# Side products woven into the quarters of each weight slab in a hybrid decoder layer

## Chip, cores and metric

One NeuronCore of a Trainium2 chip runs the whole layer in one launch. The metric is the device time of the launch in microseconds (us), as the median of several runs. The engines are called PE (TensorE), DVE (VectorE), ACT (ScalarE), POOL (GpSimd) and SP (SyncE, which issues most of the transfers).

## The reference

One decoder layer for 512 tokens of width 1024, all in float32. A normalised input `h` goes through one wide projection; its parts feed two token mixers, whose outputs are gated, summed and projected, and a squared-ReLU MLP follows:

```python
proj = h @ w_in[l]
(hq, hf, hi, hg, cq, ak, av, ik, iw, gate_a, gate_b) = jnp.split(proj, splits, axis=-1)
oa = hgrn2_mixer(hq, hf, hi, lbs[l])           # 4 heads of 128: S_t = diag(f_t) S_t-1 + (1 - f_t) i_t^T, o_t = S_t^T q_t
oa = rms_norm(oa, hgrn_norm_g) * jax.nn.silu(hg)
cq = rms_norm(cq, q_norm_g[l])
aq = cq @ w_uq[l]                              # 8 attention heads of 64
iq = cq @ w_iq[l]                              # 8 index heads of 64
ik = layer_norm(ik, ...)
ob = dsa_mixer(aq, iq, iw, ak, av, ik, rel_bias)   # score = sum_h w_h relu(iq_h . ik); top 128 keys; softmax(q.k + bias) v
mix = jax.nn.sigmoid(gate_a) * (oa @ w_up_hgrn[l]) + jax.nn.sigmoid(gate_b) * (ob @ w_up_attn[l])
x = x + mix @ w_o[l]
x = x + jnp.square(jax.nn.relu(hm @ w_mlp_in[l])) @ w_mlp_out[l]
```

## The kernel before

Each engine's instruction stream is written out by hand, and the engines meet at semaphores only: `full[b]` and `free[b]` count the uses of each of the eight PSUM banks, and named semaphores (`kk_done`, `iqh_done`, `e_done`) count steps. Float32 products are made of three fast matmuls (`three`, lines 1445 to 1447): each operand is split into a high part, rounded by a cast on ACT (`whi`, line 637), and a low part, the difference, made on DVE (`wlo`, line 956).

The weights come as slabs of 128 by 1024 numbers in the order of `PLAN`, 55 of them before the MLP. The text numbers them from 0: slabs 0 to 3 are hf, 4 to 7 hq, 8 to 11 c0, 12 c1, 13 to 16 hi, 17 iq (the index queries), 18 to 21 hg, 22 uq (the attention queries), 23 to 30 ga, 31 to 34 ua (the recurrence's up-projection), 35 to 42 gb, 43 to 46 ub and 47 to 54 wo. There are four slots for slabs. Each slab is 24 matmuls of 512 columns (of 384 in iq). The slabs write the PSUM banks 0 to 3 in rotation; everything else, the side products, writes banks 4 to 7.

The table `side[n]` names the side steps that belong to slab n; the same table drives every engine. Each engine's loop over the slabs is:

- PE: the 24 matmuls of the slab (`mms`), then the PE part of the slab's side steps.
- ACT: the high part of slab n + 3 (`hi`), then the ACT parts of the side steps, then what it does with the slab's own result (`evict`); for the slabs in `EARLY`, among them 17 (iq), 21 (hg 3) and 22 (uq), evict stands ahead of the side steps.
- DVE: the steps `diff`, `dput`, `put` of the slab, then the low part of slab n + 3 (`lo`), then side steps and evict in the same way.

The side steps that the text names:

- `mul` 0 to 6: products of the recurrence by levels; `xm` makes their operands on DVE (lines 1153 and 1154), `put` copies results into `hA`.
- `kdT`: transposes of the attention keys (`kdh`, `kdl`), and before the change also of the index keys (`ikd`, line 1088, then `ikh` on ACT and `ikl` on DVE).
- `decay_k`: DVE writes the exponents (line 1188), ACT takes the exp (line 770). `use_k` multiplies the keys `hK` by them on DVE (line 1195) and raises `kk_done`. `kT` 0 to 2 transposes `hK` on PE, the first waits for `kk_done`. `decay_q`, `use_q` and `turn` are the same for queries and `hA`. `state` and `out` are the recurrence by chunks.
- `index` 0 to 23: two matmuls, a relu on ACT and an accumulation on DVE (line 1100). `top`: one round of the top-k selection on DVE (lines 1110 and 1113), 16 rounds for each of the token tiles 1, 2 and 3.
- `on`: 16 multiplications on DVE (line 1224); `flip` and `oaT` are matmuls and transposes for what follows.
- `attn` 0 to 34, the attention of 32 (token tile, head) pairs as a pipeline: step u multiplies queries and keys of pair u on PE, adds the bias and takes the minimum on DVE (line 1241), takes the exp on ACT (line 826), transposes the pair u - 2 on PE, copies it on ACT, and multiplies the pair u - 3 by the values on PE (line 1668). Pair u - 3 lands in columns 0 to 63 of bank 7, and DVE scales it into `ob` (lines 1249 and 1252) before the next pair may be written.

Of the kernel before, what the change touches and what calls it, by code (L numbers as in the profile page):

```python
# [25 lines left out]
P = 128  # L26
# [26 lines left out]
        + [("hg", j) for j in range(4)] + [("uq", 0)] + [("ga", j) for j in range(8)] + [("ua", j) for j in range(4)]  # L53
# [21 lines left out]
def build(nc, x, slabs, vecs, consts, onehot, rel_bias, final_g, out):  # L75
    with ExitStack() as ctx:
# [6 lines left out]
        def sem(name):  # L83
# [37 lines left out]
        ikd = place("ikd", 165, T)  # L121
        ikh = place("ikh", 167, T, F32R)
# [77 lines left out]
                 "rsum_done obh_done mix_done mxh_done mxl_done hv_done hh_done hl_done fin_done rq_done "  # L200
# [89 lines left out]
        file(n_de - 1, ("decay_k",))  # L290
        file(n_de, ("put", LEVELS - 1), ("use_k",), ("decay_q",))
        file(n_de + 1, ("use_q",), ("turn",))
# [3 lines left out]
        file(n_hi + 3, ("kdT",))  # L296
        n_ch = n_de + 2
# [41 lines left out]
        N_TOP = n_top  # L339

# [289 lines left out]
        def _(act):  # L630
# [38 lines left out]
            def evict(n):  # L669
# [61 lines left out]
            def do_side(s):  # L731
# [79 lines left out]
                if k == "attn":  # L811
                    u = s[1]
                    bq, btp, bv = BK[s]
                    if btp is not None:
# [3 lines left out]
                        if v >= 2:  # L818
                            wait_full(BK["attn", v + 1][2])
# [1031 lines left out]
```

## Time and profile before

| | us |
|---|---|
| median of 3 runs (765.9 to 767.69) | 766.44 |
| the profiled execution, its own time | 767.56 |
| its span | 765.8 |
| PE busy in the span | 731.8 (96%) |
| DVE busy | 548.1 (72%) |
| ACT busy | 354.2 (46%) |

The span is the time from the first to the last instruction on the core; the profiled execution's own time is 1.8 us more. A busy PE is one that has a matmul in it; it says nothing of how fast the matmul ran.

### The profile page before, as it was taken

What the parts mean: (1) busy time and instruction counts of PE and PEld (TensorE: products, weight loads), DVE (VectorE), ACT (ScalarE), POOL (GpSimd) and SP (SyncE); (2) the same over time, 40 slices, a digit from 0 to 9 for tenths busy, and PEclk for the clock granted to TensorE, in tenths of its full rate; (3) what the DMA queues carried; (4) which work ended last, traced back from release to release, by engine and by line L of the source; (5) the groups of instructions that cost most, each with busy time, mean ns of one, the idle gap of its engine ahead of it and who ended that gap; (6) DMA issues with size and microseconds to landing.
All of it is one profiled execution on the core that took longest, in us unless ns stands there. A gap on an engine that the chain in (4) does not pass through costs nothing.

```text
span 765.8 us, 9945 instructions
## 1 busy us (share of the span) xinstructions
PE 731.8 (96%) x3498; PEld 609.8 (80%) x3498; DVE 548.1 (72%) x868; ACT 354.2 (46%) x572; POOL 84.0 (11%) x121
## 2 busy tenths in 40 slices
PE   5999999898898999999999999999999999999996
PEld 4788888687676778888888888888888888888885
DVE  4587997658999896433842677695959596868974
ACT  6463454555534334443322664535445454545442
POOL 5021330011001133420010100000000000000002
PEclk9999999899999999999999999999999999999998
DMA  7521221111222112111261515060413233241102
GB/s 286 160 89 56 69 96 56 56 55 56 84 82 83 56 56 83 56 56 56 89 244 52 195 60 185 1 194 25 164 55 129 90 101 118 82 138 55 56 1 110
DMA packets 20724, 71.51 MB, mean 93 GB/s; under 512 B 2344, under 2 KB 3536, under 8 KB 20688
## 3 DMA queue, kind: packets, MB, share of 16 engines
q1 hardware_dynamic: 19120, 67.88, 26.4%
q10 hardware_dynamic: 1568, 3.15, 1.2%
q8 instruction: 22, 0.36, 0.2%
q14 instruction: 14, 0.11, 0.0%
HBM read 68.91 MB, written 2.11 MB: 93 GB/s over the span
## 4 chain that ended last, share of the span: by engine, by line
PE 82%; DVE 13%; issue 2%; DMA 1%; ACT 1%; POOL 0%; SPq 0%; POOLq 0%; DVEq 0%
PE bank L1445 25%; PE bank L1446 24%; PE bank L1447 24%; DVE sc L1113 2%; PE bank L1668 2%; DVE small L1110 2%; DVE wlo L956 2%; PE bank L1453 1%; PE bank L1572 1%; DMA xs<-x 1%; DVE sc L1100 1%; DVE aqs L1006 1%; PE bank L1652 1%; PE bank L1653 1%; DVE hO L1224 1%
## 5 line engine op out<-in xcount | busy, mean ns | idle before, releaser
L1445 PE MATMUL bank<-hTh,whi 128*128 128x512 f32 (+1 forms) x456 | 181.1, 397 | 1.5 <-DVE hTl L976 1.5
L1447 PE MATMUL bank<-hTh,wlo 128*128 128x512 f32 (+1 forms) x456 | 178.8, 392 | 0.0
L1446 PE MATMUL bank<-hTl,whi 128*128 128x512 f32 (+1 forms) x456 | 178.6, 392 | 0.0
L1445 PEld LDWEIGHTS bank<-hTh,whi 128*128 128x128 f32 (+1 forms) x456 | 86.1, 189 | 21.3 <-issue 1.9
L956 DVE TENSOR_TENSOR wlo<-raw,whi 128x1024 fp32r<-128x1024 f32 x58 | 72.2, 1247 | 41.9 <-ACT whi L637 41.9
L1447 PEld LDWEIGHTS bank<-hTh,wlo 128*128 128x128 f32 (+1 forms) x456 | 85.8, 188 | 18.7
L1446 PEld LDWEIGHTS bank<-hTl,whi 128*128 128x128 f32 (+1 forms) x456 | 86.0, 189 | 18.2 <-issue 0.5
L637 ACT CAST whi<-raw 128x1024 fp32r<-128x1024 f32 x58 | 60.4, 1043 | 34.7 <-PE bank L1447 34.5
L1445 PE MATMUL bank<-whi,ah 128*128 128x512 f32 x196 | 76.2, 389 | 0.0
L1446 PE MATMUL bank<-wlo,ah 128*128 128x512 f32 x196 | 76.2, 389 | 0.0
L1447 PE MATMUL bank<-whi,al 128*128 128x512 f32 x196 | 76.2, 389 | 0.0
L871 ACT ACTIVATE rt<-bank 128x512 f32<-128x512 f32 x32 | 19.1, 598 | 85.9 <-PE bank L1447 85.9
L862 ACT CAST whi<-raw 128x1024 fp32r<-128x1024 f32 x29 | 29.8, 1052 | 50.3 <-PE bank L1447 50.3
L1292 DVE TENSOR_TENSOR wlo<-br,whi 128x1024 fp32r<-128x1024 f32 x32 | 39.0, 1220 | 18.8 <-ACT whi L867 18.6
L1325 DVE TENSOR_TENSOR acc<-bank,acc 128x512 f32<-128x512 f32 x70 | 44.9, 682 | 0.0
L1445 PE MATMUL bank<-whi,hTh 128*128 128x512 f32 x96 | 39.3, 410 | 3.8 <-DVE iqs L1006 3.8
L1447 PEld LDWEIGHTS bank<-whi,al 128*128 128x128 f32 x196 | 36.8, 188 | 7.7
L1445 PEld LDWEIGHTS bank<-whi,ah 128*128 128x128 f32 x196 | 36.8, 188 | 7.6
L1446 PEld LDWEIGHTS bank<-wlo,ah 128*128 128x128 f32 x196 | 36.8, 188 | 7.6
L1292 DVE TENSOR_TENSOR wlo<-raw,whi 128x1024 fp32r<-128x1024 f32 x29 | 34.8, 1219 | 10.4 <-ACT whi L862 10.4
L820 ACT ACTIVATE et<-bank 128x128 f32<-128x128 f32 (+3 forms) x32 | 14.0, 436 | 58.9 <-PE bank L1453 58.5
L1446 PE MATMUL bank<-wlo,hTh 128*128 128x512 f32 x96 | 38.5, 401 | 0.0
(231 smaller groups left out, 1360.6 us busy)
## 6 DMA issues: line engine op xcount, KB each, us to landing
raw<-slabs SPq DMA_DIRECT2D x87, 512.0 KB, 3.4
br<-slabs SPq DMA_DIRECT2D x32, 512.0 KB, 3.4
xs<-x SPq DMA_DIRECT2D x4, 512.0 KB, 5.4
y<-x ACTq DMA_DIRECT2D x1, 2048.0 KB, 8.9
out<-ys SPq DMA_DIRECT2D x3, 512.0 KB, 2.6
bt<-bias_rows ACTq DMA_DIRECT2D x1, 1024.0 KB, 5.3
cst<-consts SPq DMA_DIRECT2D x1, 608.0 KB, 9.7
fg<-final_g SPq DMA_DIRECT2D x1, 512.0 KB, 7.2
```

Source lines behind the costliest of these rows:

```text
L637: act.copy(whi[s][:, :], raw[s][:, :]).then_inc(hi_done, 1)
L862: act.copy(whi[s][:, :], raw[s][:, :]).then_inc(hi_done, 1)
L871: act.activation(rt[m % 2][:, :], bank[m][:, :], ACT.Relu).then_inc(free[m], 1)
L956: dve.tensor_tensor(wlo[s][:, :], raw[s][:, :], whi[s][:, :].bitcast(F32), ALU.subtract).then_inc(lo_done, 1)
L1110: dve.max(mx8[:, 8 * (i - 1):8 * i], sc_of(i)).then_inc(S["max_done"], 1)
L1113: dve.match_replace(sc_of(i), mx8[:, 8 * (i - 1):8 * i], sc_of(i), TAKEN).then_inc(S["rep_done"], 1)
L1292: dve.tensor_tensor(wlo[s][:, :], src[:, :], whi[s][:, :].bitcast(F32), ALU.subtract).then_inc(lo_done, 1)
L1325: dve.tensor_tensor(a_, bank[b][:, :], a_, ALU.add).then_inc(free[b], 1)
L1445: pe.matmul(dst, lh, rh, start=start, stop=False)
L1446: pe.matmul(dst, lh, rl, start=False, stop=False)
L1447: return pe.matmul(dst, ll, rh, start=False, stop=stop)
L1668: ins = pe.matmul(bank[7][:, 0:DH], et[v % 2][:, q * P:(q + 1) * P], c03[:, q, QL + GR * DH + g * DH:QL + GR * DH + (g + 1) * DH], start=q ...
```

## The change

- Every slab is cut into four parts of six matmuls each. After each part stands a share of the slab's side steps (`woven[n][p]`), on PE, ACT and DVE alike. Steps that need a bank are laid at even distances; the `top` rounds of a slab are spread over its parts. `evict` is cut in the same way, and `EARLY` is gone.
- The keys' decay moves: `decay_k` from the DVE work of slab 15 to that of slab 16, behind `kdT`; `use_k` and `decay_q` from slab 16 to the end of slab 17; `use_q` from 17 to 18. The index keys are a step of their own (`iknT`) in slab 17, with other places in memory, and no longer wait for `use_k`.
- `ga` 0 comes before `uq`: uq is now slab 23. The 24 index steps stand in slabs 18 to 21. The 35 attention steps begin at slab 31 (ua 0) and not at slab 28; they still end in slab 40. The rounds of `top` for tile 2 stand in slabs 25 to 31 (before: 23 to 29), those of tile 3 in 31 to 35 (before: 28 to 34).
- The eight heads of a token tile share bank 7: pair (i, h) is written to columns 64h to 64h + 63, and once per token tile one reciprocal of 8 columns and one multiplication of 512 columns move all of it to `ob`. PE waits for that (`ob_done`) only at the first head of the next token tile.

The diff, cut to its core (`evict`, `token_part` and `feature_part` are cut into four parts in the same way as the loops at its end):

```diff
-        + [("hg", j) for j in range(4)] + [("uq", 0)] + [("ga", j) for j in range(8)] + [("ua", j) for j in range(4)]
+        + [("hg", j) for j in range(4)] + [("ga", 0), ("uq", 0)] + [("ga", j) for j in range(1, 8)] + [("ua", j) for j in range(4)]
...
-        ikd = place("ikd", 165, T)
-        ikh = place("ikh", 167, T, F32R)
+        ikd = place("ikd", 197.5, T)
+        ikh = place("ikh", 195, T, F32R)
...
-        file(n_de - 1, ("decay_k",))
-        file(n_de, ("put", LEVELS - 1), ("use_k",), ("decay_q",))
-        file(n_de + 1, ("use_q",), ("turn",))
...
+        file(n_iq, ("iknT",))
+        file(n_de, ("put", LEVELS - 1), ("decay_k",))
+        file(n_de + 1, ("turn",), ("use_k",), ("decay_q",))
+        file(n_de + 2, ("use_q",))
...
-        spread([("index", u, i, h) for u, (i, h) in enumerate(idx_units)], n_hg, n_uq)
+        spread([("index", u, i, h) for u, (i, h) in enumerate(idx_units)], n_hg, n_hg + 3)
         file(max(n_hg + 3, n_ch + NT), ("bt", ))
-        file(n_ga, *[("on", c) for c in range(NT)])
-        spread([("flip", h) for h in range(AH // 2)], n_ga + 2, n_ga + 4)
-        file(n_ga + 4, ("oaT",))
-        spread([("attn", u) for u in range(NU + 3)], n_ga + 5, n_gb + 5)
-        spread([("top", (1,), r_) for r_ in range(rounds)], n_hg + 2, n_ga + 1)
-        spread([("top", (2,), r_) for r_ in range(rounds)], n_ga, n_ga + 6)
-        file(n_ga, ("mask", 0))
-        file(n_ga + 2, ("mask", 1))
-        file(n_ga + 7, ("mask", 2))
-        spread([("top", (3,), r_) for r_ in range(rounds)], n_ga + 5, n_gb - 1)
-        file(n_gb, ("mask", 3))
+        file(n_uq, *[("on", c) for c in range(NT)])
+        spread([("flip", h) for h in range(AH // 2)], n_ua - 6, n_ua - 4)
+        file(n_ua - 4, ("oaT",))
+        spread([("attn", u) for u in range(NU + 3)], n_ua, n_gb + 5)
+        spread([("top", (1,), r_) for r_ in range(rounds)], n_hg + 2, n_ua - 7)
+        spread([("top", (2,), r_) for r_ in range(rounds)], n_ua - 6, n_ua)
+        file(n_ua - 6, ("mask", 0), ("mask", 1))
+        file(n_ua + 1, ("mask", 2))
+        spread([("top", (3,), r_) for r_ in range(rounds)], n_ua, n_gb)
+        file(n_gb + 1, ("mask", 3))
         file(n_gb + 6, ("obT",))
 
-        EARLY = (n_hi + 3, n_iq, n_uq, n_hg + 3)
...
+                    if u == 3:
+                        pv_bank = take(7)
...
+        PARTS = 4
+        woven = {}
+        for n in range(NPLAN):
+            woven[n] = [[] for _ in range(PARTS)]
+            count = sum(s in BK for s in side[n])
+            tops = sum(s[0] == "top" for s in side[n])
+            seen, p, top = 0, 0, 0
+            for s in side[n]:
+                if s in BK:
+                    p = (2 * seen + 1) * PARTS // (2 * count)
+                    seen += 1
+                if s[0] == "top":
+                    woven[n][top * PARTS // tops].append(s)
+                    top += 1
+                else:
+                    woven[n][p].append(s)
...
             for n in range(NPLAN):
                 hi(n + AHEAD)
-                if n in EARLY:
-                    evict(n)
-                for s in side[n]:
-                    do_side(s)
-                if n not in EARLY:
-                    evict(n)
+                for p in range(PARTS):
+                    evict(n, p)
+                    for s in woven[n][p]:
+                        do_side(s)
                 for s in side[n]:
                     if s[0] == "out":
...
-                    if bv is not None:
-                        v = u - 3
-                        i, h = units[v]
-                        dve.wait_ge(S["e_done"], v + 1)
-                        if v >= 2:
-                            dve.wait_ge(free[7], BK["attn", v + 1][2][1] + 1)
-                        dve.reciprocal(resum[:, v % 2:v % 2 + 1], esum[:, v:v + 1]).then_inc(S["rsum_done"], 1)
-                        wait_full(bv)
-                        dve.wait_ge(S["rsum_done"], v + 1)
-                        dve.tensor_scalar(ob3[:, i, h * DH:(h + 1) * DH], bank[7][:, 0:DH], resum[:, v % 2:v % 2 + 1],
-                                          None, ALU.mult).then_inc(free[7], 1)
+                    if bv is not None and units[u - 3][1] == AH - 1:
+                        i = units[u - 3][0]
+                        e_ = esum[:, AH * i:AH * i + AH]
+                        dve.wait_ge(S["e_done"], AH * (i + 1))
+                        dve.reciprocal(e_, e_).then_inc(S["rsum_done"], 1)
+                        if i < NT - 1:
+                            dve.wait_ge(S["pv_done"], AH * (i + 1))
+                        else:
+                            wait_full(bv)
+                        dve.wait_ge(S["rsum_done"], i + 1)
+                        dve.tensor_tensor(ob3[:, i, :].rearrange("p (h d) -> p h d", h=AH),
+                                          bank[7][:, :].rearrange("p (h d) -> p h d", h=AH),
+                                          e_.unsqueeze(2).to_broadcast([P, AH, DH]),
+                                          ALU.mult).then_inc(S["ob_done"] if i < NT - 1 else free[7], 1)
...
-                        wait_free(bv)
+                        if v == 0:
+                            wait_free(bv)
+                        elif h == 0:
+                            pe.wait_ge(S["ob_done"], i)
...
-                mms(n)
-                for s in side[n]:
-                    do_side(s)
+                for p in range(PARTS):
+                    mms(n, p)
+                    for s in woven[n][p]:
+                        do_side(s)
 
```

DVE around the index queries, before. `hK<-hK,hX_79` is `use_k`, `wlo_57` the low part of slab 20, and the `iqs` rows free banks 0 to 3 for slab 18.

```order
L1195 TENSOR_TENSOR hK<-hK,hX_79 128x2048 [waits e1_done,xm_done,full4]
L1083 TENSOR_TENSOR kdl<-bank,kdh 128x512 [waits kdh_done] x2
L1088 TENSOR_SCALAR ikd<-bank,vec 128x512 [waits kk_done,full5]
L956 TENSOR_TENSOR wlo_57<-raw_49,whi_53 128x1024 [waits hi_done]
L1001 TENSOR_TENSOR ikl<-ikd,ikh 128x512 [waits ikh_done]
L1006 SCALAR_TENSOR_TENSOR iqs<-bank,iqs 64x384 [waits iqh_done]
L1006 SCALAR_TENSOR_TENSOR iqs<-bank,iqs 64x384
```

The same place now:

```order
L1019 SCALAR_TENSOR_TENSOR iqs<-bank,iqs 64x384 [waits iqh_done]
L1019 SCALAR_TENSOR_TENSOR iqs<-bank,iqs 64x384
L1104 TENSOR_SCALAR ikd<-bank,vec 128x512 [waits full5]
L1107 TENSOR_TENSOR ikl<-ikd,ikh 128x512 [waits ikh_done]
L1019 SCALAR_TENSOR_TENSOR iqs<-bank,iqs 64x384 [waits iqh_done]
L1019 SCALAR_TENSOR_TENSOR iqs<-bank,iqs 64x384
L1019 SCALAR_TENSOR_TENSOR iqs<-bank,iqs 64x384 [waits iqh_done]
L1019 SCALAR_TENSOR_TENSOR iqs<-bank,iqs 64x384
L1213 TENSOR_TENSOR hK<-hK,hX_79 128x2048 [waits e1_done,xm_done,full4]
L972 TENSOR_TENSOR wlo_58<-raw_50,whi_54 128x1024 [waits hi_done]
```

`use_k` stood ahead of the index keys and of all `iqs`; now it is the last row of its slab, behind all of them.

PE in slab 18 before: the last matmuls of the slab, the first key transpose, the first index product.

```order
L1445 MATMUL bank<-whi_55,hTh 128x512
L1446 MATMUL bank<-wlo_59,hTh 128x512
L1447 MATMUL bank<-whi_55,hTl 128x512
L1453 MATMUL bank<-cst,hK 128x128 [waits free4,kk_done]
L1453 MATMUL bank<-cst,hK 128x128 x3
L1562 MATMUL bank<-ikh,iqs 128x256 [waits free3,ikl_done,free2,free5,free1,free0]
L1563 MATMUL bank<-ikl,iqs 128x256
```

PE in slab 18 now:

```order
L1464 MATMUL bank<-whi_55,hTh 128x512
L1465 MATMUL bank<-wlo_59,hTh 128x512
L1466 MATMUL bank<-whi_55,hTl 128x512
L1472 MATMUL bank<-cst,hK 128x128 [waits free4,kk_done]
L1472 MATMUL bank<-cst,hK 128x128 x3
L1585 MATMUL bank<-ikh,iqs 128x256 [waits free3,ikl_done,free2,free5,free1,free0]
L1586 MATMUL bank<-ikl,iqs 128x256
L1464 MATMUL bank<-whi_55,hTh 128x512 [waits free1]
L1465 MATMUL bank<-wlo_59,hTh 128x512
```

The transposes that wait for `kk_done` stood behind all 24 matmuls of the slab; now they stand behind six of them, and 18 are queued behind them.

DVE in the attention before (slab 29). `ISA` is the minimum of line 1241, `small 128x1` reads its accumulator.

```order
L1241 ISA tt_106,small<-bank,bm_105 128x128 [waits full6,bm_done,full5]
L1241 ISA small 128x1
L1249 RECIPROCAL small<-small 128x1 [waits e_done]
L1252 TENSOR_SCALAR ob<-bank,small 128x64 [waits rsum_done,full7]
L1241 ISA tt_107,small<-bank,bm_104 128x128 [waits full6,bm_done,full4]
L1241 ISA small 128x1
L1249 RECIPROCAL small<-small 128x1 [waits e_done]
L1252 TENSOR_SCALAR ob<-bank,small 128x64 [waits rsum_done,full7]
L1241 ISA tt_108,small<-bank,bm_105 128x128 [waits full6,bm_done,full5]
L1241 ISA small 128x1
L1249 RECIPROCAL small<-small 128x1 [waits free7,e_done]
L1252 TENSOR_SCALAR ob<-bank,small 128x64 [waits rsum_done,full7]
```

DVE where the attention begins now (slab 31):

```order
L1035 SCALAR_TENSOR_TENSOR tha<-tha,bank 128x512 [waits free0,full0]
L1259 ISA tt_107,small<-bank,bm_105 128x128 [waits bm_done,full5]
L1259 ISA small 128x1
L1128 MAX small<-sc 128x8 [waits causal_done]
L1131 MATCH_REPLACE sc<-small,sc 128x512 [waits max_done]
L1259 ISA tt_108,small<-bank,bm_104 128x128 [waits bm_done,full4]
L1259 ISA small 128x1
L1128 MAX small<-sc 128x8 [waits rep_done]
L1131 MATCH_REPLACE sc<-small,sc 128x512 [waits max_done]
L1128 MAX small<-sc 128x8 [waits rep_done]
L1131 MATCH_REPLACE sc<-small,sc 128x512 [waits max_done]
L1035 SCALAR_TENSOR_TENSOR tha<-tha,bank 128x512 [waits free1,full1]
```

The reciprocals and the 64-column multiplications are gone from between the steps, and one or two rounds of the top-k selection of tile 3 (512 columns) stand between every two of them.

## Rows read from the trace of the kernel before

**Rows 1.** Waits of PE: engine, line, waited for: us, times, longest.
```profile
PE bank L1562 <- ACT hO L793: 4.2, 1, 4.2
PE bank L1668 <- DVE ob L1252: 3.8, 3, 2.3
PE bank L1445 <- DVE iqs L1006: 3.8, 1, 3.8
PE bank L1562 <- DVE hS L1214: 2.2, 2, 1.7
...
PE bank L1453 <- DVE hA L1176: 1.4, 1, 1.4
PE bank L1652 <- DVE small L1241: 1.2, 1, 1.2
```

**Rows 2.** Windows on PE: stretch, length, PE busy, granted clock, DMA.
```profile
137.33:144.15 6.82, 5.88 (x14) 0.50 0.23 77
195.35:198.77 3.42, 3.42 (x10) 0.50 0.03 2
246.55:249.97 3.42, 3.41 (x10) 0.50 0.35 138
```

**Rows 3.** Timeline of PE: first matmuls of slabs 11, 16, 43 and 44.
```profile
85.01 0.48 PE L1445 MATMUL bank<-whi,hTh 128*128 128x512 f32 x1
...
120.67 0.48 PE L1445 MATMUL bank<-whi,hTh 128*128 128x512 f32 x1
...
360.06 0.39 PE L1445 MATMUL bank<-obh,whi 128*128 128x512 f32 x1
...
365.50 0.39 PE L1445 MATMUL bank<-obh,whi 128*128 128x512 f32 x1
```

**Rows 4.** Chain of waits in order of time: side products of 8 and 16 matmuls.
```profile
68.09 0.89 PE bank L1584 x8
68.98 1.79 PE bank L1572 x16
```

**Rows 5.** Timeline of DVE from slab 10 to slab 18.
```profile
88.71 1.21 DVE L1154 TENSOR_TENSOR hX<-hX,hK 128x1024 f32<-128x1024 f32 x1
...
129.31 2.28 DVE L1195 TENSOR_TENSOR hK<-hK,hX 128x2048 f32<-128x2048 f32 x1
131.51 1.28 DVE L1083 TENSOR_TENSOR kdl<-bank,kdh 128x512 fp32r<-128x512 f32 x2
132.71 0.80 DVE L1088 TENSOR_SCALAR ikd<-bank,vec 128x512 f32<-128x512 f32 x1
...
137.00 4.59 DVE L1006 SCALAR_TENSOR_TENSOR iqs<-bank,iqs 64x384 fp32r<-64x384 f32 x8
```

**Rows 6.** Timeline of ACT: decay, index queries, the first of four squares, a slab's high part.
```profile
123.00 1.92 ACT L770 ACTIVATE hX<-hX 128x2048 f32<-128x2048 f32 x1 [10.85 <-DVE hX L1188]
...
135.02 4.05 ACT L696 ACTIVATE iqs<-bank 64x384 fp32r<-64x384 f32 x8
...
198.06 0.31 ACT L649 ACTIVATE junk<-hO 128x128 f32<-128x128 f32 x1
...
199.68 1.03 ACT L637 CAST whi<-raw 128x1024 fp32r<-128x1024 f32 x1
```

**Rows 7.** DVE from 95 to 430 us by form: busy us, mean ns, idle before.
```profile
L956 DVE TENSOR_TENSOR wlo<-raw,whi 128x1024 fp32r<-128x1024 f32 x43 | 52.9, 1229 | 40.1 <-ACT whi L637 40.1
L1110 DVE MAX8 small<-sc 128x8 f32<-128x512 f32 x16 | 11.1, 691 | 0.3
L1113 DVE MATCH_REPLACE8 sc<-small,sc 128x512 f32<-128x512 f32 x16 | 10.8, 676 | 0.0
L1252 DVE TENSOR_SCALAR ob<-bank,small 128x64 f32<-128x64 f32 x32 | 9.1, 285 | 14.9 <-PE bank L1668 14.0
...
L1006 DVE SCALAR_TENSOR_TENSOR aqs<-bank,aqs 64x512 fp32r<-64x512 f32 x8 | 5.5, 689 | 2.5 <-ACT aqs L696 2.3
...
L1224 DVE SCALAR_TENSOR_TENSOR hO<-hO,small,hSG 128x128 f32<-128x128 f32 x16 | 4.3, 348 | 0.0
...
L1241 DVE CUSTOM_DVE_ANT_0 tt<-bank,bm 128x256 f32<-128x256 f32 x8 | 3.4, 421 | 1.1 <-PE bank L1653 1.1
```

More of the change, by code:

```diff
@@ L984, in _, with evict @@
             lo(2)
-            def evict(n):
+            def evict(n, p):
                 kind, j = PLAN[n]
-                if kind == "hf":
+                last = p == PARTS - 1
+                if kind == "hf" and last:
                     b, u = tiles[n][0]
@@ L1023, in evict @@
-                if kind == "ub":
-                    for q, (b, u) in enumerate(tiles[n]):
-                        m = 2 * j + q
-                        wait_full((b, u))
-                        gb, gu = tiles[n_gb + m][0]
-                        dve.wait_ge(free[gb], gu + 1)
-                        dve.scalar_tensor_tensor(out=thb3[:, m, :], in0=thb3[:, m, :], scalar=1.0, in1=bank[b][:, :],
-                                                 op0=ALU.add, op1=ALU.mult).then_inc(free[b], 1)
+                    b, u = tiles[n][p]
@@ new lines, in evict @@
+                if kind == "ua" and p % 2:
+                    q = p // 2
+                    b, u = tiles[n][q]
+                    m = 2 * j + q
+                    wait_full((b, u))
+                    gb, gu = tiles[AT_SLAB["ga", m]][0]
+                    dve.wait_ge(free[gb], gu + 1)
+                    dve.scalar_tensor_tensor(out=tha3[:, m, :], in0=tha3[:, m, :], scalar=1.0, in1=bank[b][:, :],
+                                             op0=ALU.add, op1=ALU.mult).then_inc(free[b], 1)
@@ new lines, in evict @@
+                if kind == "ub" and p % 2:
+                    q = p // 2
+                    b, u = tiles[n][q]
+                    m = 2 * j + q
+                    wait_full((b, u))
+                    gb, gu = tiles[n_gb + m][0]
+                    dve.wait_ge(free[gb], gu + 1)
+                    dve.scalar_tensor_tensor(out=thb3[:, m, :], in0=thb3[:, m, :], scalar=1.0, in1=bank[b][:, :],
+                                             op0=ALU.add, op1=ALU.mult).then_inc(free[b], 1)
+                if kind == "ub" and last:
@@ L1041, in evict @@
                     half = j // 4
-                    if half == 0:
+                    if half == 0 and p == 0:
                         dve.wait_ge(y_in, 16)
-                    for t, (b, u) in enumerate(tiles[n]):
-                        wait_full((b, u))
-                        yy = y3[:, t, half * 512:(half + 1) * 512]
-                        dve.scalar_tensor_tensor(out=yy, in0=bank[b][:, :], scalar=0.5, in1=yy,
-                                                 op0=ALU.mult, op1=ALU.add).then_inc(free[b], 1)
+                    b, u = tiles[n][p]
+                    wait_full((b, u))
+                    yy = y3[:, p, half * 512:(half + 1) * 512]
+                    dve.scalar_tensor_tensor(out=yy, in0=bank[b][:, :], scalar=0.5, in1=yy,
+                                             op0=ALU.mult, op1=ALU.add).then_inc(free[b], 1)
             def do_side(s):
@@ L1677, in _ @@
             for n in range(NPLAN):
-                mms(n)
-                for s in side[n]:
-                    do_side(s)
+                for p in range(PARTS):
+                    mms(n, p)
+                    for s in woven[n][p]:
+                        do_side(s)
             for k in MLP_K[0:5]:
```

172 lines of the change are left out of this document (81 added, 91 removed).

## The prediction

> **What bounds the kernel now.** I read the page first: PE is busy 96% of the span, so only three things can move: PE's waits, the speed at which its matmuls run, and the number of matmuls. The change adds and removes no matmul. The list of PE's waits has 16.6 us in the six rows that belong to the projection and attention stages (4.2 + 3.8 + 3.8 + 2.2 + 1.4 + 1.2) [rows 1]; each ends with work of DVE or ACT. The windows show what follows a wait: after each of the three longest, PE's granted clock is 0.50, its lower level of 1.2 GHz, for 6.8, 3.4 and 3.4 us [rows 2]. PE is busy 5.88 + 3.42 + 3.41 = 12.7 us of that and does half as much, so 6.4 us more are lost. Together 23.0 us lie there to be won, and nothing else: the MLP is untouched.
>
> **The cuts themselves.** A slab is 24 matmuls; slab 44 begins 5.44 us after slab 43 [rows 3], 0.227 us a matmul, 1.36 us a part. Side products now stand in many short groups, not in one. A group of 8 took 0.89 us and one of 16 took 1.79 us [rows 4], 0.11 us each, so a group has no price of its own. The bound above: the first wide matmul behind a group is shown with 0.48 us, not 0.39 [rows 3], and with some 40 more groups that would be 3.6 us. I take nothing, since 8 and 16 cost the same apiece.
>
> **Slab 11.** `mul` 3 now stands behind 18 matmuls, not 24: due at 85.0 + 4.1 = 89.1 us [rows 3]. Its operand is ready when DVE ends at 88.7 + 1.2 = 89.9 [rows 5]; DVE has no pause ahead of it and its order there is the old one. A new wait of **0.8 us**. All later `mul` have over a microsecond in hand.
>
> **The keys' decay.** This is the largest term, and a loss. Everything in it is in series now, so I follow it, with the old trace's clock.
> - Slab 16 begins at 120.7 + 0.8 = 121.5 [rows 3]. 18 matmuls (4.1) and the 8 transposes of `kdT` (0.9) [rows 4] end at 126.5. ACT copies two banks, DVE ends `kdl` (0.64 the second) at 128.3 and only then writes the decay, 2.28 us as for the like row of `use_k` [rows 5]: 130.6. ACT's exp takes 1.92 [rows 6]: 132.5.
> - Behind the exp on ACT are queued the last quarter of hi's eviction, which frees bank 3 (132.9 with a copy of 0.5, as one of the eight in 4.05 us), the high part of slab 20 (1.03 [rows 6], 133.9), and all copies of the index queries. Before, ACT had the exp behind it at 124.9 and took hi's eviction at once.
> - DVE waits for that high part: low part 1.2 [rows 7] to 135.1, four `iqs` at 0.57 [rows 5] to 137.4, `ikd` 0.8 to 138.2, ACT's `ikh` 0.6 to 138.9 and its next two query copies 1.0 to 139.9, four `iqs` to 142.2, `use_k` 2.28 to **144.5**.
> - PE meanwhile: slab 16 ends at 127.9. Slab 17 is three quarters as wide (4.1 us). Its last part needs bank 3 at 131.4 and gets it at 132.9: a wait of 1.5. With `turn` (0.9) it ends at 134.8. Slab 18 needs bank 0, free after two `iqs` at 136.3: 1.4. Six matmuls later, at 137.6, the key transposes wait for `kk_done` until 144.5: **6.9 us**. In sum 9.8, where the old kernel waits 1.4 + 3.8 = 5.2 [rows 1]. 18 matmuls of slab 18 that used to stand ahead of those transposes are queued behind them.
>
> **The index steps, uq and ga 0.** The waits of 4.2 (`hO`, ahead of an index product) and 2.2 (`hS`) [rows 1] go: a part of 1.36 us of wide matmuls now stands between two side steps, and `out` no longer follows its `state` at once. They leave two at uq. From the end of slab 22: tanh 0.6, four squares 1.6, high part 1.0 [rows 6], two query copies 1.2, two `aqs` 1.4 [rows 7] give 5.9 with the semaphores, and slab 24 wants their bank after 5.4: 0.6. Then DVE does the 16 `on` (4.3), a round (1.0) and two `aqs` (1.4) [rows 7] before slab 25 gets its bank, 12.6 against 11.4: 1.2. Together **1.8 us**. The transfer of the bias rows is issued some 6 us earlier and is waited for by `flip` two slabs later, as before: nothing.
>
> **The attention.** The waits of 3.8 (`ob`) and 1.2 (`small`) [rows 1] go where they were. The multiplication to `ob`, 9.1 us in 32 pieces [rows 7], becomes four; of the new form I have only the nearest rows, 0.69 for 512 columns [rows 7], four times 0.7 with a reciprocal. But the start moves to slab 31, into the same slabs as the rounds for tile 3. DVE in slabs 31 to 35: 5 low parts of 1.2 (6.0); 16 rounds of 0.69 + 0.68 + 0.13 for the match load and the handover (24.0); 2 rounds of tile 2 (2.5); 18 minima, from 0.37 to 0.64 by width, 0.42 + 0.08 for 256 columns (8.2); 8 gate products at 0.69 (5.5); one `ob` and a mask (1.2): **47.4 us** [rows 7]. PE there: five slabs (27.2) and 18 attention steps of 5 to 11 small matmuls, 0.6 to 1.2 us each (15): 42.2. PE cannot run ahead, since step u transposes what DVE gave for u - 2. So PE waits **5.2 us** in many pieces of a microsecond or so. Ahead of slab 31 there are no minima, and by the prices of [rows 7] I estimate some 85 us of work for DVE in slabs 18 to 30, less than PE has, so DVE is not late when the stage begins; behind slab 35 the rounds are over and PE leads again. The three waits for `ob_done` come with a quarter slab between: nothing; bound above 3 x 0.9.
>
> **The clock.** Where PE was idle 3.8 us the low level ran on for 5.9 us of work [rows 2]. What the wait of 6.9 brings is not in the trace: nothing if the level comes back while PE waits, 3.4 us if all 6.8 us of the low level fall on work. I take 1.7. A rule of the Trainium skill speaks against this change here (TensorE: Matmul & The Clock Gate, section "Why this matters for your kernels": idle gaps between bursts of matmuls should be avoided, for after one the array is back at half its clock). Our three windows agree with it; read strictly it makes this term 3.4 and the time 764.4.
>
> **The sum.** Lost before 23.0. Lost after 0.8 + 9.8 + 1.8 + 5.2 + 1.7 = 19.3. Gain 3.7 us. The profiled execution took 767.6 (span 765.8 and 1.8 around it), 1.1 above the median of the runs shown; the change is taken off both: 763.9 for such an execution, **762.7 for the median**. For a measurement of this kernel 0.2% (1.5 us) is about what can be told from no change.
>
> **The rivals.**
> - The keys are no late arrival (0.11). If ACT and DVE run through the chain some 7 us faster than I add up, the transposes find `kk_done` raised, and the clock stays up: 762.7 - 6.9 - 1.7 = 754.1. For it: handovers between engines are in my sum by guess. Against it: twelve operations in series, each with a row. It decides if `use_k` ends before 137.6 on the old clock.
> - The clock stays low longer (0.18). The long wait costs 3.4 and one of the waits in slabs 31 to 35 adds a stretch of 3.4 us at the low level (1.7), as the 2.3 us wait before 246 did [rows 1, 2]: 766.1. Against it: no wait of under 2 us had that effect in the old trace.
> - Every cut costs (0.05). The 0.09 us of the first wide matmul is real loss: 762.7 + 3.6 = 766.3.
> - The attention goes in series (0.13), slower. In slabs 31 to 35 PE waits for DVE's minimum and ACT's exp, and DVE then waits for PE's next product instead of working through: half of the 18 steps lose 0.6 us more, 5.4, and one clock stretch 1.7: 769.8. It decides at 5.3 us beyond my 5.2, or 0.3 a step. For it: PE waited on this chain before where rounds stood between steps (3.8 and 1.2). Against it: DVE has a round to do beside every wait.
> - The forecast case (0.53): 759.5 to 766 by itself.
>
> **How the numbers follow.** Of the forecast case 0.49 lie below 764.9 and 0.04 near no change; the fast rival adds 0.11, and of the clock rival 0.05: 0.65 faster. Within 0.2%: 0.04 + 0.11 + 0.04 = 0.19. Slower: 0.13 and the rest of clock and cuts, 0.16. The range reaches down halfway to the fast rival, 757, and up to 768.5, between the clock rival and the serial one.
>
> **What the new profile would show.** PE's waits: one of 6 to 7 us on the key transposes, released by DVE's write of `hK`, in slab 18; the rows for `hO`, `hS` and `iqs` gone or under 1.5 us; waits of about 1 us on `aqs`; many short ones between slabs 31 and 35 released by line 1259's minimum or ACT's `tt`. DVE over 95% busy in that stretch, and PE about 90%. A low clock once, at the key transposes. The attention's end (slab 41) comes some 4 us earlier than before. The prediction is wrong if the key transposes wait under 3 us, if the stage of slabs 31 to 35 takes under 45 or over 52 us, or if the clock is low for over 10 us in all.

## The result, and the profile after

The changed kernel takes 761.67 us (median of 4 runs, 760.92 to 763.04), the one before, run beside it, 766.28 us (4 runs, 765.9 to 767.69): a ratio of 0.9939, 95% interval 0.992 to 0.9958. The profiled execution took 763.04 us with a span of 761.3. The forecast was 762.7 (757 to 768.5).

First PE's list of waits after the change (idle time in total, times, longest):

```profile
PE bank L1472 <- DVE hK L1213: 6.7, 1, 6.7
PE bank L1472 <- ACT et L838: 2.8, 5, 1.0
PE bank L1694 <- DVE ob L1271: 1.7, 1, 1.7
...
PE bank L1464 <- DVE aqs L1019: 1.4, 2, 0.9
PE bank L1464 <- ACT hV L722: 1.3, 1, 1.3
PE bank L1464 <- DVE iqs L1019: 1.2, 1, 1.2
PE bank L1675 <- DVE small L1259: 0.9, 1, 0.9
```

Against [rows 1], `hO` (4.2) and `hS` (2.2) are gone, `iqs` has shrunk from 3.8 to 1.2, `ob` from 3.8 to 1.7, and in their place stands one wait of 6.7 us on the key transposes, and five short ones on `et`.

Then the windows (stretch, length, busy time of PE, PEld, DVE, ACT, POOL, granted clock, DMA): slabs 16 to 40, the first low-clock stretch, slabs 31 to 35, and the second low-clock stretch.

```profile
121.47:342.80 221.33, 205.31 (x1092) 173.13 (x1090) 154.86 (x342) 110.54 (x240) 41.03 (x59) 0.98 0.20 66
141.31:148.14 6.83, 3.44 (x11) 3.00 (x12) 6.53 (x6) 4.42 (x6) 0.00 (x0) 0.50 0.13 35
241.98:290.17 48.19, 42.78 (x226) 35.53 (x224) 41.45 (x105) 19.26 (x57) 12.58 (x20) 0.96 0.17 58
274.43:277.84 3.41, 3.41 (x10) 2.69 (x9) 3.34 (x10) 0.60 (x2) 0.73 (x1) 0.50 0.49 154
```

The same slabs 16 to 40 took 226.64 us before, with PE busy 209.53, so they are 5.3 us shorter; slabs 0 to 15 are 0.4 us longer (106.12 against 105.72), the rest equal. PE works 3.4 + 3.4 us at the low clock, where it worked 12.7 [rows 2].

For all kernels I made the same account from PE's timeline: the time T from the first matmul of slab 0 to the first of the MLP; the sum of PE's gaps over 0.06 us in it; half of PE's busy time at clock 0.50, as the cost of the low clock; and the rest. All in us.

| kernel | T | gaps | low clock | rest |
|---|---|---|---|---|
| before | 414.6 | 17.6 | 6.3 | 390.7 |
| changed | 409.7 | 16.5 | 3.4 | 389.8 |
| e6, one bank alone | 412.9 | 15.9 | 7.6 | 389.3 |
| e3, no weaving | 410.9 | 13.5 | 7.9 | 389.5 |
| e1, decay back | 403.3 | 11.9 | 1.7 | 389.7 |
| e2, slab 18's steps late | 405.3 | 12.9 | 1.7 | 390.7 |
| e5, both | 399.6 | 9.5 | 0.0 | 390.1 |
| e4, attention from 28 | 409.8 | 17.8 | 3.2 | 388.8 |
| e7, rounds over six slabs | 396.8 | 6.9 | 0.0 | 389.9 |
| e8, rounds over seven slabs | 397.7 | 8.1 | 0.0 | 389.6 |
| e12, e7 with attention from 29 | 399.2 | 7.4 | 3.2 | 388.6 |
| e9, e7 without weaving | 403.8 | 10.4 | 3.4 | 390.0 |
| e10, e7 with `on` later | 395.6 | 6.0 | 0.0 | 389.7 |
| e11, the changed kernel again | 409.6 | 16.6 | 3.3 | 389.8 |

Half is a little too much for the low clock. Before, at clock 0.50, wide matmuls follow each other after 0.43 us, against 0.227 at full clock [rows 3], so 47% of the time is lost, 1.6 us and not 1.7 of a stretch of 3.41:

```profile
197.66 0.63 PE L1446 MATMUL bank<-hTl,whi 128*128 128x512 f32 x1
198.09 0.63 PE L1447 MATMUL bank<-hTh,wlo 128*128 128x512 f32 x1
```

So the change won 1.1 us of gaps, 2.9 of low clock and 0.9 in the rest, 4.9 in all (by the 47%: 1.1, 2.7 and 1.1). The gaps mostly moved. Each row of the table is one execution, and the low clock varies between executions of one kernel: the 39 timed runs of the kernel before that stand beside the experiments go from 764.91 us (mean granted clock 0.994) to 769.2 us (0.985). The low-clock column is therefore one draw of several. Nor is the rest a constant: it goes from 388.6 to 390.7, so that differences in it of under 1 us prove little by themselves.

### The profile page after: what moved, and what is told of

It reads as the page before. It is cut to its first block, busy times and chain, and to the rows that moved or that the text cites. A ratio compares the mean times of both kernels' runs of the same rounds, so it can differ in the third digit from the quotient of the medians.

```text
span 761.3 us, 9803 instructions
## 1 busy us (share of the span) xinstructions
PE 728.4 (96%) x3498; PEld 606.7 (80%) x3498; DVE 537.6 (71%) x812; ACT 357.5 (47%) x572; POOL 84.5 (11%) x121
## 4 chain that ended last, share of the span: by engine, by line
PE 89%; DVE 6%; ACT 2%; issue 2%; DMA 1%; SPq 0%; POOL 0%; POOLq 0%; ACTq 0%; DVEq 0%
PE bank L1464 26%; PE bank L1466 26%; PE bank L1465 26%; PE bank L1694 2%; PE bank L1472 2%; PE bank L1595 2%; DMA xs<-x 1%; DVE small L1128 1%; DVE sc L1131 1%; ACT whi L655 1%; DVE iqs L1019 1%; PE bank L1586 1%; PE bank L1585 1%; DVE hO L1242 1%; DVE tha L1035 1%
## 5 line engine op out<-in xcount | busy, mean ns | idle before, releaser
L972 DVE TENSOR_TENSOR wlo<-raw,whi 128x1024 fp32r<-128x1024 f32 x58 | 74.7, 1289 | 57.7 <-ACT whi L655 57.4
L1311 DVE TENSOR_TENSOR wlo<-raw,whi 128x1024 fp32r<-128x1024 f32 x29 | 34.8, 1218 | 10.5 <-ACT whi L878 10.5
L1466 PE MATMUL bank<-whi,hTl 128*128 128x512 f32 x96 | 37.8, 393 | 0.0
```

What stands on the lines that cost most here:

```text
L972: dve.tensor_tensor(wlo[s][:, :], raw[s][:, :], whi[s][:, :].bitcast(F32), ALU.subtract).then_inc(lo_done, 1)
L1311: dve.tensor_tensor(wlo[s][:, :], src[:, :], whi[s][:, :].bitcast(F32), ALU.subtract).then_inc(lo_done, 1)
L1466: return pe.matmul(dst, ll, rh, start=False, stop=stop)
```

## The experiments

Ratios are to runs of the kernel before on the same chip (medians 768.2, 767.6 and 767.8 us for the three groups e1 to e3 with e6; e4, e5, e7, e8; e9 to e12), with 95% intervals. In the edits, a line `...` marks what is left out.

### e6_bank_alone: one part of the change alone

The kernel before, with only the shared bank 7 for a tile's heads and one multiplication to `ob`:

```
+                    if u == 3:
+                        pv_bank = take(7)
...
-                             take(7) if u >= 3 else None)
+                             pv_bank if u >= 3 else None)
```

> The kernel before with one part of the change alone: the eight heads of a token tile share bank 7 and are scaled once. Theory A (VectorE is late there because of the selection rounds, so the wait passes from the scaling to the minima): waits of 3.8 us become 2 to 3 on the minima, 764 to 766 us. Rival B (the scaling itself is the wait): the 3.8 us and the stretch of low clock of 1.7 us go, 760.8 us.

764.54 us, ratio 0.9949 (0.9931 to 0.9967). Its waits:

```profile
PE bank L1567 <- ACT hO L795: 4.2, 1, 4.2
PE bank L1450 <- DVE iqs L1008: 3.8, 1, 3.8
PE bank L1657 <- DVE small L1243: 2.6, 3, 1.6
PE bank L1567 <- DVE hS L1216: 2.3, 2, 1.8
```

The wait on `ob` is gone and that on `small`, the minimum, grew from 1.2 to 2.6. By the account the rest fell by 1.4 us and the gaps by 1.6, and the low clock cost 1.3 more. The shared bank alone gives 0.5% where the whole change gives 0.6%: all its other parts together net about nothing, as far as these intervals tell, and the next experiments show why. The time lies in theory A's range, but the kernel before took 768.2 us on this chip and not 766.4: the gain of 3.9 us lies between the two theories. The wait did pass to the minima, as A says, at a smaller price.

### e3_no_weave: the changed kernel without the weaving

```
+        woven = {n: [[], [], [], list(side[n])] for n in range(NPLAN)}
```

> The changed kernel with all side steps of every slab behind its 24 matmuls: the new places of the steps and the shared bank without the weaving. Theory A (weaving is what took away the waits on hO and hS, and costs no more matmul time): those waits come back with 4 to 7 us, the wait on the keys shrinks by 4 to 6, the waits of slabs 31 to 35 stay about 5: 761 to 766 us. Rival B (short groups of side products cost TensorE time of their own, 0.09 us each): 3 us faster than by that sum, 758 to 761 us, with the summed spacing of matmuls lower.

762.42 us, ratio 0.9926 (0.9908 to 0.9944): no different from the changed kernel.

```profile
PE bank L1676 <- DVE small L1260: 4.9, 3, 3.7
PE bank L1465 <- DVE iqs L1020: 3.7, 1, 3.7
PE bank L1586 <- DVE hS L1233: 2.3, 2, 1.8
```

There is no wait on `hK` and none on `hO` here. The first is covered by slab 18's 24 matmuls. The second is gone without any weaving, so the new order of the steps is enough for it; the likely reason is that the index steps now end in slab 21, and none stands behind the last `out`. Of the two, only `hS` is the weaving's. The gaps are 3.0 us less than in the changed kernel, the low clock costs 7.9 us and not 3.4. So the weaving's gain and what it does to the key transposes cancel; e9 shows the gain without the late keys.

### e1_decay_back: the keys' decay where it was

```
+        file(n_de - 1, ("decay_k",))
+        file(n_de, ("put", LEVELS - 1), ("use_k",), ("decay_q",))
...
-        file(n_de, ("put", LEVELS - 1), ("decay_k",))
-        file(n_de + 1, ("turn",), ("use_k",), ("decay_q",))
-        file(n_de + 2, ("use_q",))
+        file(n_de + 1, ("turn",), ("use_q",))
```

> The changed kernel with the keys' decay where it was before (decay in slab 15, the multiplication of the keys and the queries' exp in slab 16), all else as changed. Theory A (the decay's place makes the chain to the key transposes): the wait of 6.7 us on the keys is gone; next late is the first index product in slab 18, which needs all eight parts of the index queries freed by VectorE, some 3 to 4 us, and bank 0 some 1.5 us; 757 to 759 us, with no stretch of low clock or a shorter one. Rival B (the decay's place costs nothing, the wait only shows which semaphore came last): the same 761.7 us, the wait under another name at full length.

756.36 us, ratio 0.9853 (0.9836 to 0.9871), some 6.5 us below the changed kernel by the two ratios, and 0.6 below theory A's range. Rival B falls. Its waits in the stages concerned:

```profile
PE bank L1585 <- DVE iqs L1019: 3.8, 1, 3.8
PE bank L1472 <- ACT et L838: 2.8, 5, 1.0
PE bank L1694 <- DVE ob L1271: 1.7, 1, 1.7
```

The 6.7 us on `hK` and both waits on banks ahead of it are gone, and 3.8 us on the index queries, which was hidden behind them, comes up.

### e2_late_sides: nothing queued behind the key transposes

The decay stays late, but in slab 18 the side steps stand behind all 24 matmuls.

```
+        woven[n_hg] = [[], [], [], list(side[n_hg])]
```

> The changed kernel, but in slab 18 alone all side steps stand behind the 24 matmuls, as before the change; the decay stays late. Theory A (the loss is that 18 matmuls are queued behind the waiting transposes): the wait on the keys falls to 1 us or less, a wait of some 1.5 us on banks 2 and 3 appears within the slab, sum of waits down by 4 us, 756 to 758 us. Rival B (the keys come late whatever stands ahead of them, so the time comes back later in the recurrence): 761 us or more.

757.56 us, ratio 0.9864 (0.9843 to 0.9884). Slabs 16 to 18 take 25.5 us, not 30.9. The wait on `hK` is 0.4 us. So 5.4 us of the loss come from the 18 matmuls behind the transposes. The late decay has a price of its own beside it: with it undone as well (e5, below) the same slabs take 22.5 us, 3.0 less. The waits that are left here are those on banks of slabs 17 and 18 (1.3 on `hV`, 3.1 on `iqs`) and 0.8 on `rel`.

### e5_both: e1 and e2 together

> The changed kernel with the keys' decay back in slabs 15 to 17 and, besides, the side steps of slab 18 all behind its 24 matmuls. Theory A (each edit alone took 4 to 5 us, and what e1 has left is one wait of 3.8 us on the index queries' low parts with a clock stretch of 3.4 us behind it): the 24 matmuls cover most of that wait; short waits on banks of slabs 17 and 18 of about 3 us in all stay. Time 753 to 755.5, no wait on an index product over 1 us. Rival B (both edits cover the same chain, so the second adds nothing): 756 to 757, as e1 alone.

754.28 us, ratio 0.9825 (0.9809 to 0.9841). The longest wait before slab 31 is this one, and slabs 16 to 18 take 22.5 us:

```profile
PE bank L1465 <- DVE iqs L1020: 1.4, 1, 1.4
```

No low clock shows in the profiled execution (752.7 us). Two of the five runs took 752.7 and 752.9, three 754.3 to 754.6. The distance, 1.6 us, is what one stretch of 3.41 us costs, and the mean granted clock of the runs goes the same way (0.998 and 0.997 for the two, 0.996 for the three). No trace of a slower one was kept, so the stretch itself isn't shown.

### e4_attn_28: the attention begins three slabs earlier

```
-        spread([("attn", u) for u in range(NU + 3)], n_ua, n_gb + 5)
+        spread([("attn", u) for u in range(NU + 3)], n_ua - 3, n_gb + 5)
...
-        file(n_gb + 1, ("mask", 3))
+        file(n_gb, ("mask", 3))
```

> The changed kernel with the attention's 35 steps spread from slab 28 on instead of slab 31 (mask of tile 3 one slab earlier); the 16 rounds for tile 3 stay in slabs 31 to 35. Theory A (the 5.4 us of waits in slabs 31 to 35 and the 1.7 us wait for ob are DVE's load: 24 us of rounds in five slabs, whatever stands beside them): fewer attention steps stand beside the rounds (14, not 18), DVE loses 2 us and PE 3, so PE still waits 4 to 7 us there: 760 to 763.5. Rival B (it is the late start, that is, how densely the steps stand, that makes PE wait): 2.7 steps a slab and not 3.5 leave under 2 us of waits in the whole attention: 756 to 758.

766.0 us (12 runs, 762.95 to 767.12), ratio 0.9974 (0.9962 to 0.9987). The profiled execution, 762.95 us, reaches slab 41 at 342.65, as the changed kernel does (342.80). Its short waits are gone, and `ob` has them all:

```profile
PE bank L1694 <- DVE ob L1271: 6.4, 2, 4.1
PE bank L1675 <- DVE oal L992: 0.4, 1, 0.4
```

So PE must wait for DVE somewhere, and an earlier start only chooses where. Theory B falls. The median is above what I expected: the 12 times lie in two groups, 763.0 to 764.1 and 765.8 to 767.1, and the profile is of the lower one. The mean granted clock goes with the groups: 0.989 to 0.991 in the four runs of the lower one, 0.984 to 0.987 in the eight of the upper. So the upper group had more low clock, enough for the 3 us if it fell on work; where in the kernel it came no trace shows.

### e7_rounds_six: fewer rounds beside the attention

As e5, with tile 3's rounds over slabs 31 to 36.

```
-        spread([("top", (3,), r_) for r_ in range(rounds)], n_ua, n_gb)
+        spread([("top", (3,), r_) for r_ in range(rounds)], n_ua, n_gb + 1)
```

> As e5_both, and the 16 rounds for tile 3 are spread over six slabs (31 to 36), not five. Theory A (DVE's load in slabs 31 to 35): 2.7 rounds of 1.5 us leave the stage, 4.0 us of DVE, and slab 36, where DVE is under half busy, takes them for nothing. PE's waits between slabs 31 and 35 fall from 5.4 to 1 to 2.5 us and the one on ob to under 0.5; the time is 2.5 to 5 us below e5_both. Rival B (the waits come from the chain minimum, exp, transpose inside a step): nothing changes, within 1 us of e5_both.

749.88 us (749.62 to 750.39), ratio 0.9771 (0.9756 to 0.9786), 4.4 us below e5. Of these 2.8 show between the two profiled executions (T 399.6 and 396.8), neither of which has a low clock; 1.6 is the distance between e5's two groups. Its windows of slabs 31 to 35 and of slab 36:

```profile
233.38:277.06 43.68, 40.92 (x225) 34.24 (x224) 37.60 (x98) 18.20 (x56) 11.99 (x20) 1.00 0.18 62
277.06:286.50 9.44, 9.44 (x58) 8.29 (x57) 7.51 (x19) 5.67 (x14) 4.62 (x8) 1.00 0.16 57
```

Its waits of PE and DVE in slabs 31 to 35:

```profile
DVE wlo L973 <- ACT whi L656: 5.4, 4, 1.8
...
PE bank L1473 <- ACT et L839: 2.0, 4, 1.0
...
PE bank L1695 <- DVE ob L1272: 0.3, 1, 0.3
```

DVE's work in the stage fell by 3.9 us (41.45 to 37.60), the stage by 4.5 (48.2 to 43.7; 1.6 of it e5 had already, with 46.6, where the low clock was missing), and slab 36 took those rounds with PE busy all the time. Rival B falls: DVE's load sets most of what PE waits in this stage. The 2.0 us on `et` are still there.

### e8_rounds_seven: one slab earlier too

```
-        spread([("top", (3,), r_) for r_ in range(rounds)], n_ua, n_gb)
+        spread([("top", (3,), r_) for r_ in range(rounds)], n_ua - 1, n_gb + 1)
```

> As e7_rounds_six, but over seven slabs (30 to 36), so that 11.4 rounds and not 13.3 stand in slabs 31 to 35, and 2.3 in slab 30, where DVE was 70% busy. Theory A: another 1 to 2 us less of waits, at most 1 us of waits left in slabs 31 to 36: 4 to 6.5 us below e5_both. Rival B: as e5_both within 1 us. Third case: slab 30 makes DVE late at the stage's start, and the gain over e7_rounds_six is nothing or negative.

750.74 us, ratio 0.9788 (0.9772 to 0.9804). The third case: PE waits 1.0 us on a minimum already in slab 31, and 1.7 on `ob`. Theory A falls. That with DVE this full a round put earlier makes DVE late earlier fits the wait in slab 31; why the one on `ob` is 1.7 again, with fewer rounds ahead of it than in e7 (0.3), isn't shown.

### e12_six_attn_29: e7 with an earlier attention

```
-        spread([("attn", u) for u in range(NU + 3)], n_ua, n_gb + 5)
+        spread([("attn", u) for u in range(NU + 3)], n_ua - 2, n_gb + 5)
```

> As e7_rounds_six, but the attention's 35 steps begin in slab 29, so 2.9 and not 3.5 stand in a slab. Theory A (only DVE's sum counts, and the rounds set it): the waits change their places, to ob above all as in e4_attn_28, and the time is 749 to 751.5. Rival B (with the rounds eased, the density of the steps is what is left of the waits, 2.7 us): 747 to 748.5.

751.96 us, ratio 0.9794 (0.9777 to 0.9812), just above A's range. First its longest wait in the attention, then the window of the low clock behind it:

```profile
PE bank L1695 <- DVE ob L1272: 3.3, 1, 3.3
```

```profile
253.47:260.30 6.83, 6.35 (x21) 5.61 (x22) 5.42 (x14) 2.85 (x8) 1.73 (x3) 0.50 0.03 11
```

The waits sum to little more than in e7 (gaps 7.4 us against 6.9), but they are one of 3.3 us, and a low clock follows it for 6.83 us, 3.2 us lost. Several short waits were cheaper here than one long one.

### e9_six_no_weave: what the weaving is worth

The line of e3, in e7.

> As e7_rounds_six (749.9 us), but in every slab all side steps stand behind the 24 matmuls. It asks what the weaving is worth once the keys' decay and the rounds for tile 3 are not late. Theory A (the cuts cost nothing and keep PE fed): the waits on hS and small that e3_no_weave had come back, 5 to 8 us of waits and a clock stretch or two: 756 to 760. Rival B (weaving is worth nothing, as e3 against the changed kernel suggests): 749 to 751.5. In between, the waits of the profile have to say.

756.54 us, ratio 0.9851 (0.9831 to 0.987), some 6 us above e7 by the two ratios. Its waits:

```profile
PE bank L1676 <- DVE small L1260: 2.7, 2, 2.1
PE bank L1586 <- DVE hS L1233: 2.4, 2, 1.8
PE bank L1473 <- DVE hA L1195: 1.4, 1, 1.4
```

Of the 7.0 us between the two T, 3.6 are gaps and 3.4 low clock. The rest is the same (390.0 against 389.9), so the cuts cost nothing in sum. With the keys cured, the weaving of the other slabs is worth some 6 us, more than the shared bank alone (3.9 in e6); with the keys late (e3) it is worth nothing.

### e10_on_later: one more queue cleared

```
-        file(n_uq, *[("on", c) for c in range(NT)])
+        file(n_uq + 1, *[("on", c) for c in range(NT)])
```

> As e7_rounds_six, but the 16 products to hO of the side steps `on` (4.3 us of DVE) stand one slab later, in slab 24, behind the low parts of the aqs. By the chain of the prediction, the wait of 0.9 us ahead of slab 25 is DVE's 4.3 us of `on` in front of the last two aqs: it goes, the one of 0.6 us ahead of slab 24 stays. 748.8 to 749.4, at best just told apart. Rival: those products only move in front of something else that PE waits for (the flips or oaT), and the time is 749.9 or more.

748.82 us (748.57 to 748.91), ratio 0.9759 (0.9742 to 0.9775). The wait ahead of slab 25 is gone, that ahead of slab 24 is there:

```profile
PE bank L1465 <- DVE aqs L1020: 0.6, 1, 0.6
```

This is the fastest version: 13.7 us below the changed kernel as e11 timed it on the same chip, and 2.4% below the one before.

### e11_changed_again: the changed kernel once more

> The changed kernel once more, for its time on the same chip as the others and for a second profile: is the low clock behind the 1.7 us wait on ob there in each execution? Theory A: the second stretch comes and goes, and each stretch of 3.4 us of a low clock is worth 1.7 us, so that the times fall in groups 1.7 us apart: 760 to 764. Rival: it is there always, and all times are within 1 us.

762.52 us (6 runs, 761.65 to 762.84), ratio 0.9936 (0.992 to 0.9952). Every wait of its profile is within 0.1 us of the first one's, and the low clock is there twice, 6.83 and 3.41 us long. Theory A falls here: the times are not in groups. They spread over 1.2 us, a little more than the rival's 1 us. Whether the second stretch came in each execution, two profiles can't tell.

## Why the prediction was right, step by step

**The whole.** Predicted gain 3.7 us of 766.4, measured 4.7 by the ratio. The sign and the size were right; below, what each term did. That the whole came within 1 us of the forecast is in part luck: the clock took 1.7 us more than its term, the other terms together took 1.2 less than theirs, and 1.7 us were won that the sum didn't hold.

**The cuts** (taken at nothing): right, by e9 against e7 and e3 against the changed kernel in the account's last column (390.0 and 389.9, 389.5 and 389.8). The first wide matmul with 0.48 us costs nothing that the account shows.

**Slab 11** (0.8): 0.3. The chain of waits shows one group of 16 longer than its like:

```profile
82.54 1.78 PE bank L1595 x16
89.78 2.05 PE bank L1595 x16
```

The operand was ready at 89.7, not 89.9. The other 0.1 us of slabs 0 to 15 I can't place, but it is the weaving's: slabs 0 to 15 take 105.7 us in e3 and e9, as before, and 106.1 here.

**The keys' decay** (9.8: 1.5 + 1.4 + 6.9): 9.2 (1.3 + 1.2 + 6.7). Timelines, first of DVE from slab 16 to 18, then of ACT:

```profile
128.20 2.28 DVE L1206 TENSOR_TENSOR hX<-hF 128x2048 f32<-128x2048 f32 x1
133.89 1.22 DVE L972 TENSOR_TENSOR wlo<-raw,whi 128x1024 fp32r<-128x1024 f32 x1 [3.40 <-ACT whi L655]
135.14 2.28 DVE L1019 SCALAR_TENSOR_TENSOR iqs<-bank,iqs 64x384 fp32r<-64x384 f32 x4
...
140.04 2.28 DVE L1019 SCALAR_TENSOR_TENSOR iqs<-bank,iqs 64x384 fp32r<-64x384 f32 x4 [0.33 <-ACT iqs L712]
142.35 2.29 DVE L1213 TENSOR_TENSOR hK<-hK,hX 128x2048 f32<-128x2048 f32 x1
```

```profile
130.52 1.91 ACT L788 ACTIVATE hX<-hX 128x2048 f32<-128x2048 f32 x1 [3.06 <-DVE hX L1206]
132.34 0.58 ACT L722 ACTIVATE hV<-bank 128x512 f32<-128x512 f32 x1
132.81 1.04 ACT L655 CAST whi<-raw 128x1024 fp32r<-128x1024 f32 x1
```

Read it as the prediction did: DVE's decay ends at 130.5 (forecast 130.6), ACT's exp at 132.4 (132.5), bank 3 is free at 132.9 (132.9), the low part ends at 135.1 (135.1), four `iqs` at 137.4 (137.4), the last `iqs` at 142.3 (142.2), `use_k` at 144.6 (144.5). Twelve operations in series came out within 0.1 us. The `3.40` is the cost of the order: DVE stands idle while ACT takes the exp, because the low part it wants is queued on ACT behind it. e1 and e2 show the cause by two separate cures.

**Index steps, uq and ga 0** (1.8): 1.4 (0.56 + 0.88). e10 shows the second to be DVE's `on`, as said. That `hO` and `hS` would go was right. The prediction named both the weaving and the order; e3 shows that for `hO` the order does it alone, and for `hS` the weaving is needed.

**The attention** (5.2): 3.7 in six short gaps, and 1.7 on `ob`, together 5.4. I had given `ob_done` nothing, with a bound of 0.9 each; that term was mis-sized. The short waits came to 1.5 less than the 5.2, so it is luck that the sum agrees. Timeline of DVE there:

```profile
268.97 0.41 DVE L1259 CUSTOM_DVE_ANT_0 tt<-bank,bm 128x256 f32<-128x256 f32 x1
...
270.12 0.68 DVE L1131 MATCH_REPLACE8 sc<-small,sc 128x512 f32<-128x512 f32 x1
270.71 0.68 DVE L1035 SCALAR_TENSOR_TENSOR tha<-tha,bank 128x512 f32<-128x512 f32 x1
271.30 0.42 DVE L1259 CUSTOM_DVE_ANT_0 tt<-bank,bm 128x256 f32<-128x256 f32 x1
271.64 0.20 DVE L1265 RECIPROCAL small<-small 128x8 f32<-128x8 f32 x1
271.95 0.69 DVE L1271 TENSOR_TENSOR ob<-bank,small 128x512 f32<-128x512 f32 x1
```

The tile's last value product starts on PE at 268.85; DVE comes to `ob` at 271.95, since it has two minima, a round and a gate product to do first. The quarter slab between the steps (1.36 us) helps only if DVE keeps pace. In e7, with fewer rounds, the same wait is 0.3.

The stage of slabs 31 to 35 took 48.2 us, and I had counted 47.4 of DVE work. That agreement is in part luck. DVE was busy 41.5 us, 86% and not over 95%: the durations of its 105 instructions do add up to 46.5 us, near the 47.4, but they overlap (a round is 0.69 + 0.09 + 0.68 by its rows, and the next instruction starts 1.39 us after it began). What I left out is DVE's own wait there. First the row of DVE's waits, then the timeline of both engines around one of the four:

```profile
DVE wlo L972 <- ACT whi L655: 5.4, 4, 1.8
```

```profile
262.10 0.28 DVE L1259 CUSTOM_DVE_ANT_0 tt<-bank,bm 128x128 f32<-128x128 f32 x1
...
262.43 0.40 ACT L844 ACTIVATE tt<-tt,small 128x128 f32<-128x128 f32 x1 [1.54 <-DVE small L1259]
262.74 0.19 ACT L844 ACTIVATION_READ_ACCUMULATOR tt<-tt,small 128x1 f32 x1
262.83 1.03 ACT L655 CAST whi<-raw 128x1024 fp32r<-128x1024 f32 x1
...
263.89 1.22 DVE L972 TENSOR_TENSOR wlo<-raw,whi 128x1024 fp32r<-128x1024 f32 x1 [1.23 <-ACT whi L655]
```

At a slab's start ACT must take the exp of the last step before it makes the next slab's high part, and the exp waits for DVE's minimum, so DVE, next in line for the low part, waits for work that is queued on ACT behind the answer to its own last minimum: 4 times, 5.4 us. In e7, with less work for DVE, it is 5.4 again, so it comes of the order in the queues and not of how late DVE is. Busy 41.5 and 5.4 make 46.9 of the 48.2; in e7 37.6 and the same 5.4 make 43.0 of 43.7. That a low part placed later in DVE's queue would win these 5.4 us is argued from the rows and wasn't tried.

**The clock** (1.7): 3.4. The stretch at the key transposes was as taken: 6.83 us long, half of it on an idle PE, 1.7 us lost. A second one came behind the wait on `ob`, also 1.7. This is one half of the rival "The clock stays low longer": its other half, 3.4 us at the long wait, didn't come. I had held it back with "no wait of under 2 us had that effect in the old trace"; in the new one a stretch follows a wait of 1.7. The stretches add up to 10.2 us, just over the 10 that I had named as a sign of error, though half of the first fell on an idle PE. So by its own sign the clock term failed, and the forecast held in spite of it. By the pitch of the wide matmuls (0.43 against 0.227 us) the "half as much" of the forecast was a little high too: the 6.4 us that lay there were 5.9. The Trainium skill (TensorE: Matmul & The Clock Gate, section "Why this matters for your kernels") has a rule against long idle gaps between bursts of matmuls. The wait of 6.7 us agrees with it; the one of 1.7 us is shorter than the gaps that it warns of, and a stretch at the low clock followed it all the same. No stretch followed the two of 1.3 and 1.2 us ahead of slab 18.

**The other signs.** Slab 41 begins 4.5 us earlier (342.80 against 347.31; I had said 4), and PE was 89% busy in slabs 31 to 35 (90). The short waits there end with ACT's copy `et`, not its `tt`.

**What the sum left out.** The terms as measured make 0.4 + 9.2 + 1.4 + 5.4 + 3.4 = 19.8, a gain of 3.2 against the 23.0; the account shows 4.9. Of the 1.7 between them, 0.4 are five gaps of about 0.1 us in the old attention that [rows 1] doesn't hold, and 1.3 lie in the account's rest, which fell by 0.9 although slabs 0 to 15 grew by 0.4. In e6 it fell by 1.4, 1.2 of it in slabs 28 to 40, where the attention of the kernel before stands; so it most likely belongs to the shared bank. Which of the attention's steps it comes from I can't show. That nothing lay outside the 23.0 was wrong by that much.

## What to carry to other kernels

Cutting side work in between matmuls cost PE nothing here (390.0 us of work without the cuts, 389.9 with them), but it puts matmuls behind each side step's wait: before weaving a slab, look at what each step waits for, and leave the late ones at its end. Where one engine is full, count its work per stage, move part of it to the next stage with room, and expect an earlier start of its consumers only to move the wait. Follow a chain through two engines in queue order, other work queued in front included: here twelve operations came out within 0.1 us.

## What the runs showed of the hardware

Ahead of the MLP, every stretch of the low clock (0.50) in the fourteen profiles was 3.41 or 6.83 us long. Which one, and whether at all, doesn't follow from the wait's length: 3.8 us brought 6.83 before and 3.41 in e1; 3.3 us brought 6.83 in e12, 4.1 us 3.41 in e4. A 1.7 us wait on `ob` brought 3.41 in the changed kernel (both profiles) and in e2, and none in e5 and e8; one of 1.8 us on `hS` brought 3.41 in e3, e6 and e9, and one of 1.7 none before. In e7 and e10, where the waits were all under 1.5 us, the profiles show no low clock ahead of the MLP, and the times of repeated runs lay within 0.8 and 0.3 us, against 1.2 to 4.2 us for the kernels with longer waits.
